# Seven quadrant products in fifteen column pairs of the up projection instead of eight

## The chip, the cores and the metric

The kernel runs on one core of one Trainium2 chip. The metric is the device time of one execution in microseconds, the median over several executions. The engines are TensorE (PE; its weight loads are PEld), VectorE (DVE), ScalarE (ACT), GpSimd (POOL) and SyncE (SP), which issues the transfers.

## The reference, cut to what matters

One layer of a decoder trunk for 512 tokens of width 1024 in float32. The change touches one product of it, the up projection of the channel-mixing part, whose output has 2 x 2816 columns:

```python
u = jnp.einsum('bsd,df->bsf', x, w_up[l])          # (512 x 1024) @ (1024 x 5632)
u_gate, u_val = jnp.split(u, 2, axis=-1)
a = jax.nn.gelu(causal_depthwise_conv(u_gate, w_conv[l], b_conv[l]), approximate=False) * u_val
ffn = jnp.einsum('bsf,fd->bsd', a, w_down[l])
```

## The kernel before

**Split products.** Every float32 operand of TensorE is held as a high part (rounded by ScalarE to fp32r) and a low part (the rest, a subtraction). `split_product` (line 1279 issues its matmuls) makes three matmuls for each product: high by high, high by low, low by high. For the streamed weights ScalarE writes the high part, `w_hi`, and GpSimd the low part, `w_lo`, in two subtractions of 128x512 (line 465).

**The stream.** Weights come as blocks of 128x1024, 512 KB each, through four slots. SP issues the load of a block when `block_done` says that TensorE is through with the block four places ahead of it.

**Column pairs.** The up projection is cut into `FB` = 22 pairs, numbered f = 0 to 21. A pair is a gate block and an up block, each 1024 keys by 128 columns, for the same 128 columns. A plain pair (`plain_up` on TensorE) is 2 blocks x 8 key tiles x 3 matmuls = 48 matmuls with 512 tokens each. ScalarE then reads the gate bank with scale and bias (`gate_conv`, line 761), VectorE adds the other two taps (`taps`, line 1145, two instructions), ScalarE takes the gelu (line 768), and VectorE multiplies by the up bank into `aT` (line 1153 or 1162). `act_ready` counts these products and frees the banks.

**Seven products.** In eight pairs (f = 5, 7, ..., 19) the pair's product is cut into quadrants (gate or up columns, lower or upper half of the keys, left or right half of the tokens) and made from seven products with sums of quadrants, by the Strassen-Winograd scheme, in place of eight. Each of the seven is 4 key tiles x 3 matmuls = 12 matmuls with 256 tokens, so 84 for the pair. The token sums `s_*` are made once. For every such pair the other engines make:
- VectorE: four weight sums `t_raw` of 128x512 (`w_sum`, line 1210; both inputs lie in SBUF, the on-chip memory), in the order 1, 2, 4, 3, and four additions of partial results of 128x256, `ps` and `p_copy` (lines 1221 to 1227);
- ScalarE: the high parts `t_hi` of the four sums (line 781), four copies of partial results out of PSUM, the matmul's output memory (`copy`, line 801), and the high parts of the gate block (line 786) and of half the up block (line 791);
- GpSimd: the low parts `t_lo` of the four sums (line 511), and the low parts of three quadrants of the weights: `b11_lo` (line 517), a quarter of the up block into `w_hi` (line 520) and the second gate quarter (line 526).

TensorE takes the products in the order P1 (sum 1), P2 (`b11`), P3 (the second gate quarter), P4 (sum 2), P5 (up block), P6 (sum 3), P7 (sum 4).

A plain pair runs ahead of each of the eight in one loop body, in which the seven-product pair has its fixed slots (`GATE_SLOT`, `UP_SLOT`) and fixed banks. Sums 2, 4 and 3 of a seven-product pair are made while TensorE works on the plain pair ahead of it. `t_raw` and `t_lo` of a sum share their memory. Each engine takes its instructions strictly in the written order.

Of the kernel before, what the change touches and what calls it, by code (L numbers as in the profile page):

```python
# [21 lines left out]
P = 128  # L22
# [98 lines left out]
def layer(nc, xT, x_tok, w_stream, w_out, cols, rows, square, out):  # L121
# [90 lines left out]
    t_raw = {m: at(f"t_raw{m}", [P, 512], f32, area_a + (50 + 2 * m) * K) for m in range(1, 5)}  # L212
# [28 lines left out]
    def plain(ap):  # L241

        return ap.bitcast(f32)

    with ExitStack() as ctx:
# [60 lines left out]
        p_done, p_copied, b21_lo = sem("p_done"), sem("p_copied"), sem("b21_lo")  # L306
# [35 lines left out]
        GATE_SLOT, UP_SLOT = (N_UP + 2) % 4, (N_UP + 3) % 4  # L342
        C11, C21, C12, C22 = (ps[:, c:c + HALF] for c in (1024, 1024 + HALF, 3 * 512, 5 * 512))
# [11 lines left out]
        def _(sp):  # L355
# [73 lines left out]
            assert n_loop == S_END  # L429
            for n in range(N_UP + 4, N_UP + 4 + 4 * S_FROM):  # L430
                load_when_free(n)
            with sp.Fori(S_FROM, S_END) as i:
# [27 lines left out]
        def _(pool):  # L460
# [43 lines left out]
            for n in range(N_UP + 2, N_UP + 4 * S_FROM + 2):  # L504
                low(n, n % 4)
            def sum_low(i, m):

                pool.wait_ge(t_hi_done, 4 * i + (SUMS.index(m) + 1 - 4 * S_FROM))
                if m in (1, 2):
                    pool.wait_ge(t_summed, 4 * i + (m + 1))  # L510
# [12 lines left out]
            def up_low(i, more):
                sum_low(i, 1)
                pool.wait_ge(t_summed, 4 * i + 3)
                nc.gpsimd.tensor_tensor(w_lo[:, GATE_SLOT, 512:1024], w_raw[:, GATE_SLOT, 512:1024],
                                        plain(w_hi[:, GATE_SLOT, 512:1024]), ALU.subtract).then_inc(b21_lo, 1)
                for m in (2, 3, 4):
                    sum_low(i, m)
                for j in range(4, 6):  # L530
                    low(4 * i + (N_UP + j), (N_UP + j) % 4)
                if more:
                    quarters_low(i + 1)

            quarters_low(S_FROM)
            with pool.Fori(S_FROM, S_END - 1) as i:
                up_low(i, True)
            up_low(S_END - 1, False)
            first = N_UP + 4 * S_END + 2
# [12 lines left out]
        def _(act):  # L552
# [226 lines left out]
            def w_sum_high(i, m):  # L779
                act.wait_ge(t_summed, 4 * i + (SUMS.index(m) + 1))  # L780
                nc.scalar.activation(t_hi[m][:], t_raw[m][:], ACT.Copy).then_inc(t_hi_done, 1)  # L781

            def gate_high(i):
                arrived(None, GATE_SLOT, i + (N_UP + 2) // 4)
                act.wait_ge(block_done, 4 * i + (N_UP - 1))
                nc.scalar.activation(w_hi[:, GATE_SLOT, :], w_raw[:, GATE_SLOT, :], ACT.Copy).then_inc(hi_ready, 1)

            def up_quarter_high(i):
                arrived(None, UP_SLOT, i + (N_UP + 3) // 4)
                act.wait_ge(block_done, 4 * i + N_UP)  # L790
# [12 lines left out]
            def up_high(i, more):

                for m in SUMS[1:]:
                    w_sum_high(i, m)
                act.wait_ge(block_done, 4 * i + (N_UP + 1))
                gate_conv(2 * i, 0)
                copy(i, 0, C12)
                next_high(i, 4)  # L810
                copy(i, 1, C22)
                gate_gelu(2 * i, 0)
                next_high(i, 5)
                copy(i, 2, C22)
                copy(i, 3, C22)
                if more:
                    gate_high(i + 1)
                act.wait_ge(gate_done, i + (1 - S_FROM))
                gate_conv(2 * i + 1, 1)
                if more:  # L820
                    up_quarter_high(i + 1)
                    w_sum_high(i + 1, 1)
                gate_gelu(2 * i + 1, 1)
# [15 lines left out]
            plain_up(3)  # L839
            gate_high(S_FROM)  # L840
            up_quarter_high(S_FROM)
            w_sum_high(S_FROM, 1)
            with act.Fori(S_FROM, S_END - 1) as i:
                up_high(i, True)
            up_high(S_END - 1, False)
            high_in_order(N_DOWN - 2)
            high_in_order(N_DOWN - 1)
            act.wait_ge(p_done, 5 * N_S)
# [30 lines left out]
        def _(dve):  # L879
# [320 lines left out]
            def w_sum(i, m):  # L1200

                b11, b21 = (w_raw[:, GATE_SLOT, 512 * k:512 * (k + 1)] for k in range(2))
                b12, b22 = (w_raw[:, UP_SLOT, 512 * k:512 * (k + 1)] for k in range(2))
                a, b = {1: (b12, b11), 2: (b22, t_raw[1][:]), 4: (b21, t_raw[2][:]), 3: (b22, b12)}[m]
                if m == 1:
                    for slot in (GATE_SLOT, UP_SLOT):
                        dve.wait_ge(raw_in[slot], 16 * i + (16 * ((N_UP + 2 + (slot == UP_SLOT)) // 4) + 16))
                else:
                    dve.wait_ge(t_summed, 4 * i + SUMS.index(m))
                nc.vector.tensor_tensor(t_raw[m][:], a, b, ALU.subtract).then_inc(t_summed, 1)  # L1210

            def up_products(i, more):

                count = i + (1 - S_FROM)
                for m in SUMS[1:]:
                    w_sum(i, m)
                taps(2 * i, 0)
                times_up(2 * i, 0, block_done, 4 * i + (N_UP + 2))
                dve.wait_ge(p_copied, 4 * i + (3 - 4 * S_FROM))
                dve.wait_ge(block_done, 4 * i + (N_UP + 4))  # L1220
                nc.vector.tensor_tensor(C12, C12, p_copy[:, 2, :], ALU.add).then_inc(up_left, 1)
                dve.wait_ge(p_copied, 4 * i + (4 - 4 * S_FROM))
                nc.vector.tensor_tensor(C22, C22, p_copy[:, 0, :], ALU.add).then_inc(up_right, 1)
                dve.wait_ge(p_done, 5 * i + (5 - 5 * S_FROM))
                nc.vector.tensor_tensor(C11, C11, p_copy[:, 1, :], ALU.add).then_inc(gate_left, 1)
                dve.wait_ge(gate_left, count)
                nc.vector.tensor_tensor(C21, C21, p_copy[:, 3, :], ALU.add).then_inc(gate_done, 1)
                if more:
                    w_sum(i + 1, 1)
                taps(2 * i + 1, 1)  # L1230
                times_halves(2 * i + 1, count)
# [444 lines left out]
```

## Time and profile before

| | us |
|---|---|
| median of 3 executions (lowest, highest) | 740.76 (740.60, 740.86) |
| the profiled execution, its own time | 741.66 |
| its span from the first to the last instruction | 739.9 |
| TensorE busy | 729.7 (99%) |
| VectorE, ScalarE, GpSimd busy | 427.9, 366.6, 383.1 |

The seven-product stretch runs from 433.81 us (the first matmul of pair 5) to 590.75 us (the first of pair 20). Busy times of matmuls overlap, so their spacing is read from the starts in the timeline and not from the mean duration. GB/s and clocks are for the whole stretch that a row names.

### The profile page before, as it was taken

The numbers are of one execution on the slowest core, as the hardware profiler recorded it, in microseconds if no ns is written. First come the engines' busy times: TensorE is split into PE (matmuls) and PEld (weight loads), VectorE is DVE, ScalarE is ACT, GpSimd is POOL, SyncE is SP. The second block draws the span as 40 slices with busy tenths as digits, with TensorE's granted clock in tenths as the row PEclk, the third lists the DMA queues.
The fourth block names the chain that finished last, engine by engine and source line by source line (L and its number), as shares of the span: only waits on it lengthen the run. The fifth ranks groups of instructions, "written<-read, shape, count | busy, mean of one in ns | idle before, by whom it ended". The sixth has DMA issues, their size and how long they took to land.

```text
span 739.9 us, 10440 instructions
## 1 busy us (share of the span) xinstructions
PE 729.7 (99%) x3763; PEld 623.9 (84%) x3763; DVE 427.9 (58%) x609; ACT 366.6 (50%) x525; POOL 383.1 (52%) x268
## 2 busy tenths in 40 slices
PE   8999999999999999999999999999999999999995
PEld 6888888888888888888898898888999988888884
DVE  3329579879889674446568545555444442322567
ACT  4325786876787775661125344544445343323410
POOL 6645245525525434981007577666667652845800
PEclk9999999999999999999999999999999999999998
DMA  8323414214124213661003332232323327222002
GB/s 304 112 100 117 126 55 112 90 58 143 58 80 119 86 58 140 258 231 54 0 1 114 106 123 85 85 108 90 113 85 113 113 86 284 99 100 85 28 29 85
DMA packets 24480, 78.36 MB, mean 106 GB/s; under 512 B 2944, under 2 KB 3328, under 8 KB 24448
## 3 DMA queue, kind: packets, MB, share of 16 engines
q1 hardware_dynamic: 24448, 77.94, 31.2%
q8 instruction: 20, 0.33, 0.2%
q14 instruction: 12, 0.10, 0.0%
HBM read 71.63 MB, written 2.10 MB: 100 GB/s over the span
## 4 chain that ended last, share of the span: by engine, by line
PE 94%; ACT 2%; DVE 2%; issue 1%; DMA 0%; POOL 0%; DVEq 0%; SPq 0%; POOLq 0%
PE ps L1279 92%; PE ps L1381 2%; PE ps L1462 0%; DMA w_raw<-w_stream_in 0%; POOL w_lo L465 0%; ACT fx_p L664 0%; DVE fx_p L988 0%; DVE sb_t L997 0%; DVE sb_lo L881 0%; DVE sb_t L1028 0%; ACT k_bias_rows L614 0%; ACT sb_t L658 0%; DVE fx_p L1025 0%; ACT sb_hi L688 0%; ACT sb_t L653 0%
## 5 line engine op out<-in xcount | busy, mean ns | idle before, releaser
L465 POOL TENSOR_TENSOR w_lo<-w_raw,w_hi 128x512 fp32r<-128x512 f32 x186 | 260.1, 1425 | 267.8 <-ACT w_hi L568 261.6
L568 ACT ACTIVATE w_hi<-w_raw 128x1024 fp32r<-128x1024 f32 x92 | 97.0, 1056 | 106.9 <-DMA w_raw<-w_stream_in 106.5
L1279 PE MATMUL ps<-x1T_hi,w_hi 128*128 128x512 f32 (+1 forms) x312 | 109.7, 352 | 0.0
L1279 PE MATMUL ps<-x1T_lo,w_hi 128*128 128x512 f32 (+1 forms) x312 | 109.6, 351 | 0.0
L1279 PE MATMUL ps<-xT_hi,w_hi 128*128 128x512 f32 x264 | 105.2, 399 | 0.0
L1279 PE MATMUL ps<-xT_lo,w_hi 128*128 128x512 f32 x264 | 102.9, 390 | 0.0
L1279 PE MATMUL ps<-x1T_hi,w_lo 128*128 128x512 f32 (+1 forms) x280 | 100.4, 359 | 0.0
L1279 PE MATMUL ps<-xT_hi,w_lo 128*128 128x512 f32 x256 | 100.0, 391 | 0.0
L881 DVE TENSOR_TENSOR a_lo<-aT,a_hi 128x512 fp32r<-128x512 f32 x22 | 32.9, 1511 | 64.2 <-ACT a_hi L756 64.2
L1279 PEld LDWEIGHTS ps<-x1T_hi,w_hi 128*128 128x128 f32 x312 | 59.1, 189 | 7.7
L1279 PEld LDWEIGHTS ps<-x1T_lo,w_hi 128*128 128x128 f32 x312 | 59.1, 189 | 7.4
L1279 PEld LDWEIGHTS ps<-x1T_hi,w_lo 128*128 128x128 f32 x280 | 52.9, 189 | 7.9
L1279 PEld LDWEIGHTS ps<-xT_lo,w_hi 128*128 128x128 f32 x264 | 49.7, 188 | 9.4
L1279 PEld LDWEIGHTS ps<-xT_hi,w_hi 128*128 128x128 f32 x264 | 49.6, 188 | 9.3
L1279 PEld LDWEIGHTS ps<-xT_hi,w_lo 128*128 128x128 f32 x256 | 48.0, 188 | 10.2
L1279 PE MATMUL ps<-w_hi,a_hi 128*128 128x512 f32 x136 | 52.9, 389 | 0.0
L1279 PE MATMUL ps<-w_lo,a_hi 128*128 128x512 f32 x136 | 52.9, 389 | 0.0
L1279 PE MATMUL ps<-w_hi,a_lo 128*128 128x512 f32 x136 | 52.9, 389 | 0.0
L511 POOL TENSOR_TENSOR t_lo<-t_raw,t_hi 128x512 fp32r<-128x512 f32 x32 | 44.8, 1420 | 15.3 <-DVE t_raw L1210 15.3
L1145 DVE SCALAR_TENSOR_TENSOR conv<-ps,col,conv 128x511 f32<-128x511 f32 (+1 forms) x44 | 32.9, 748 | 31.7 <-ACT conv L761 29.4
L801 ACT ACTIVATE p_copy<-ps 128x256 f32<-128x256 f32 x32 | 12.3, 385 | 50.5 <-PE ps L1279 49.6
L781 ACT ACTIVATE t_hi<-t_raw 128x512 fp32r<-128x512 f32 x32 | 20.2, 630 | 20.9 <-DVE t_raw L1210 20.1
(193 smaller groups left out, 1563.6 us busy)
## 6 DMA issues: line engine op xcount, KB each, us to landing
w_raw<-w_stream_in SPq DMA_DIRECT2D x109, 512.0 KB, 3.2
wout_raw<-w_out_in SPq DMA_DIRECT2D x8, 512.0 KB, 4.7
r_raw<-w_stream_in SPq DMA_DIRECT2D x5, 512.0 KB, 9.2
xT_raw<-xT_in SPq DMA_DIRECT2D x8, 256.0 KB, 7.0
x<-x_tok_in SPq DMA_DIRECT2D x4, 512.0 KB, 4.1
ln_rows<-rows_in SPq DMA_DIRECT2D x4, 512.0 KB, 5.7
out_dram<-x SPq DMA_DIRECT2D x8, 256.0 KB, 2.0
sb_q<-sb_q SPq DMA_DIRECT2D x8, 128.0 KB, 2.4
```

The source lines that it names most:

```text
L465: lo = nc.gpsimd.tensor_tensor(w_lo[:, slot, cs], w_raw[:, slot, cs], plain(w_hi[:, slot, cs]), ALU.subtract)
L511: nc.gpsimd.tensor_tensor(t_lo[m][:], t_raw[m][:], plain(t_hi[m][:]), ALU.subtract).then_inc(t_split, 1)
L568: nc.scalar.activation(w_hi[:, slot, :], w_raw[:, slot, :], ACT.Copy).then_inc(hi_ready, 1)
L781: nc.scalar.activation(t_hi[m][:], t_raw[m][:], ACT.Copy).then_inc(t_hi_done, 1)
L801: nc.scalar.activation(p_copy[:, k, :], place, ACT.Copy).then_inc(p_copied, 1)
L881: return nc.vector.tensor_tensor(out_lo, whole, plain(part_hi), ALU.subtract)
L1145: nc.vector.scalar_tensor_tensor(conv[:, j, t:SEQ], ps[:, 512 * 2 * j:512 * (2 * j + 1) - t], col[:, ds(f * CONV_WIDTH + (COL_CW + CONV_WI ...
L1279: return nc.tensor.matmul(out_, lhs, rhs, start=start, stop=stop, skip_group_check=True)
L1381: last = nc.tensor.transpose(ps[:, o:o + P], weights[:, QUERY_OFF[r] + P * c:QUERY_OFF[r] + P * (c + 1)], ident[:])
```

## The change

All fifteen pairs f = 5 to 19 are made with seven products. Banks and slots follow from f (`quarters_of`, `slot_of`): even and odd pairs have bank sets of their own. `t_raw` has memory of its own, and so has the low part of the second gate quarter (`b21_lo`). The loops now cover four pairs a round, three rounds (f = 6 to 17), with the rest written out. In the new bodies ScalarE (`up_high`), VectorE (`up_products`) and GpSimd (`up_low`, `seven_low`) work for three pairs in turn: the one before (f0 - 1), the present one (f0) and the next (f0 + 1). The final multiplication is two instructions of 256 tokens. GpSimd makes the low part of `b11` for pair f0 + 1 after P3 of pair f0 is done, since `b11_lo` is one buffer.

The core of the diff, mostly the added side; the replaced functions are those printed above:

```diff
+S_FIRST, S_LAST, ROUND = 5, 19, 4
+LOOP = S_FIRST + 1
+ROUNDS = (S_LAST + 1 - LOOP) // ROUND
...
+def by_seven(f):
+    return S_FIRST <= f <= S_LAST
+def sevens_ahead(f):
+    return sum(map(by_seven, range(f)))
+N_S = sevens_ahead(FB)
...
+    t_raw = {m: at(f"t_raw{m}", [P, 512], f32, area_g + (14 + 2 * m) * K) for m in range(1, 5)}
...
+    b21_lo = at("b21_lo", [P, 512], f32r, area_c)
...
+        def block_of(f0, i):
+            return 8 * i + (N_UP + 2 * f0)
+        def count_of(f0, i, each, k=0):
+            return ROUND * each * i + (each * sevens_ahead(f0) + k)
+        def slot_of(f0, g):
+            return (N_UP + 2 * f0 + g) % 4
+        def turn_of(f0, i, g):
+            return 2 * i + (N_UP + 2 * f0 + g) // 4
+        def quarters_of(f0):
+            j = f0 % 2
+            starts = 1024 * j, 1024 * j + HALF, 1024 * j + 512, (4 + j) * 512
+            return (ps[:, c:c + HALF] for c in starts)
...
+            def sum_low(f0, i, m):
+                pool.wait_ge(t_hi_done, count_of(f0, i, 4, m))
                 nc.gpsimd.tensor_tensor(t_lo[m][:], t_raw[m][:], plain(t_hi[m][:]),
                                         ALU.subtract).then_inc(t_split, 1)
...
+            def seven_low(g0, i):
+                gate, up = slot_of(g0, 0), slot_of(g0, 1)
+                pool.wait_ge(hi_ready, block_of(g0, i) + 1)
+                if by_seven(g0 - 1):
+                    pool.wait_ge(block_done, block_of(g0 - 1, i) + 1)
+                nc.gpsimd.tensor_tensor(b11_lo[:], w_raw[:, gate, 0:512], plain(w_hi[:, gate, 0:512]),
+                                        ALU.subtract).then_inc(lo_ready, 1)
+                pool.wait_ge(hi_ready, block_of(g0, i) + 2)
+                nc.gpsimd.tensor_tensor(w_hi[:, up, 0:512], w_raw[:, up, 512:1024], plain(w_hi[:, up, 512:1024]),
+                                        ALU.subtract).then_inc(lo_ready, 1)
+                sum_low(g0, i, 1)
+                nc.gpsimd.tensor_tensor(b21_lo[:], w_raw[:, gate, 512:1024], plain(w_hi[:, gate, 512:1024]),
+                                        ALU.subtract).then_inc(b21_split, 1)
+                sum_low(g0, i, 2)
+            def up_low(f0, i):
+                if by_seven(f0):
+                    sum_low(f0, i, 3)
+                    sum_low(f0, i, 4)
+                if by_seven(f0 + 1):
+                    seven_low(f0 + 1, i)
+                else:
+                    for g in range(2):
+                        low(block_of(f0 + 1, i) + g, slot_of(f0 + 1, g))
+            pool.sem_inc(t_split, 4)
+            for f in range(LOOP):
+                up_low(f, 0)
...
+            def w_sum_high(f0, i, m):
+                act.wait_ge(t_summed, count_of(f0, i, 4, SUMS.index(m) + 1))
+                act.wait_ge(p_done, count_of(f0, i, 5, (1, 3, 4, 5)[m - 1]))
                 nc.scalar.activation(t_hi[m][:], t_raw[m][:], ACT.Copy).then_inc(t_hi_done, 1)
...
+            def next_high(f0, i, g):
+                slot = slot_of(f0, g)
+                own = slice(512, 1024) if g == 1 and by_seven(f0) else slice(0, 1024)
+                arrived(None, slot, turn_of(f0, i, g))
+                act.wait_ge(block_done, block_of(f0, i) + (g - 3))
+                nc.scalar.activation(w_hi[:, slot, own], w_raw[:, slot, own], ACT.Copy).then_inc(hi_ready, 1)
+            def copy(f0, i, k, place):
+                act.wait_ge(p_done, count_of(f0, i, 5, 6 + k))
                 nc.scalar.activation(p_copy[:, k, :], place, ACT.Copy).then_inc(p_copied, 1)
...
+            def up_high(f0, i):
+                before, now, after = map(by_seven, (f0 - 1, f0, f0 + 1))
+                c11, c21, c12, c22 = quarters_of(f0)
+                last = 4 * i + (f0 - 1)
+                if now:
+                    w_sum_high(f0, i, 4)
+                if before:
+                    act.wait_ge(gate_done, count_of(f0 - 1, i, 1, 1))
+                else:
+                    act.wait_ge(block_done, block_of(f0 - 1, i) + 1)
+                gate_conv(last, (f0 - 1) % 2)
+                if now:
+                    copy(f0, i, 0, c12)
+                    copy(f0, i, 1, c22)
+                gate_gelu(last, (f0 - 1) % 2)
+                next_high(f0 + 1, i, 0)
+                if now:
+                    copy(f0, i, 2, c22)
+                next_high(f0 + 1, i, 1)
+                if after:
+                    w_sum_high(f0 + 1, i, 1)
+                    w_sum_high(f0 + 1, i, 2)
+                if now:
+                    copy(f0, i, 3, c22)
+                if after:
+                    w_sum_high(f0 + 1, i, 3)
...
+            def times_halves(f, j, count):
...
+                _, _, c12, c22 = quarters_of(j)
+                for t, ready, part in ((0, up_left, c12), (1, up_right, c22)):
+                    dve.wait_ge(ready, count)
+                    cs = slice(HALF * t, HALF * (t + 1))
+                    half_done = nc.vector.tensor_tensor(aT[:, ds(f, 1), cs].rearrange("p o c -> p (o c)"), part,
+                                                        gelu[:, j, cs], ALU.mult)
+                half_done.then_inc(act_ready, 1)
...
+            def w_sum(f0, i, m):
+                gate, up = slot_of(f0, 0), slot_of(f0, 1)
+                b11, b21 = (w_raw[:, gate, 512 * k:512 * (k + 1)] for k in range(2))
+                b12, b22 = (w_raw[:, up, 512 * k:512 * (k + 1)] for k in range(2))
...
+                    for g in range(2):
+                        dve.wait_ge(raw_in[slot_of(f0, g)], 16 * turn_of(f0, i, g) + 16)
...
+                    dve.wait_ge(t_summed, count_of(f0, i, 4, SUMS.index(m)))
+                dve.wait_ge(t_split, count_of(f0, i, 4, m))
                 nc.vector.tensor_tensor(t_raw[m][:], a, b, ALU.subtract).then_inc(t_summed, 1)
...
+            def up_products(f0, i):
+                before, now, after = map(by_seven, (f0 - 1, f0, f0 + 1))
+                last, j = 4 * i + (f0 - 1), (f0 - 1) % 2
+                if before:
+                    c11, c21, _, _ = quarters_of(f0 - 1)
+                    dve.wait_ge(p_done, count_of(f0 - 1, i, 5, 10))
+                    nc.vector.tensor_tensor(c11, c11, p_copy[:, 1, :], ALU.add).then_inc(gate_left, 1)
+                    dve.wait_ge(gate_left, count_of(f0 - 1, i, 1, 1))
+                    nc.vector.tensor_tensor(c21, c21, p_copy[:, 3, :], ALU.add).then_inc(gate_done, 1)
+                taps(last, j)
+                if after:
+                    w_sum(f0 + 1, i, 1)
+                if before:
+                    times_halves(last, j, count_of(f0 - 1, i, 1, 1))
+                else:
+                    times_up(last, j, block_done, block_of(f0 - 1, i) + 2)
+                if after:
+                    w_sum(f0 + 1, i, 2)
+                    w_sum(f0 + 1, i, 4)
+                _, _, c12, c22 = quarters_of(f0)
+                if now:
+                    dve.wait_ge(p_copied, count_of(f0, i, 4, 3))
+                    dve.wait_ge(block_done, block_of(f0, i) + 2)
+                    nc.vector.tensor_tensor(c12, c12, p_copy[:, 2, :], ALU.add).then_inc(up_left, 1)
+                if after:
+                    w_sum(f0 + 1, i, 3)
+                if now:
+                    dve.wait_ge(p_copied, count_of(f0, i, 4, 4))
+                    nc.vector.tensor_tensor(c22, c22, p_copy[:, 0, :], ALU.add).then_inc(up_right, 1)
...
+                pe.wait_ge(act_ready, 4 * i + (f0 + 1))
...
+                    up(block_of(f0, i) + g, slot_of(f0, g), 2 * (f0 % 2) + g, 0, SEQ)
+            def seven_products(f0, i):
...
+                def sum_ready(m):
+                    pe.wait_ge(t_split, count_of(f0, i, 4, m + 4))
...
+                    pe.wait_ge(p_copied, count_of(f0, i, 4, k))
+                c11, c21, c12, c22 = quarters_of(f0)
+                gate, up_ = slot_of(f0, 0), slot_of(f0, 1)
+                pe.wait_ge(act_ready, 4 * i + (f0 + 1))
...
+                times(c12, t_hi[1], t_lo[1], s_hi[1], s_lo[1], True).then_inc(p_done, 1)
+                weight_ready(block_of(f0, i))
+                times(c22, w_hi[:, gate, 0:512], b11_lo, *x_parts(0, 0), True).then_inc(p_done, 1)
+                pe.wait_ge(b21_split, count_of(f0, i, 1, 1))
+                pe.wait_ge(t_summed, count_of(f0, i, 4, 3))
+                times(c11, w_hi[:, gate, 512:1024], b21_lo, *x_parts(1, 0), True).then_inc(block_done, 1)
...
+                times(c22, t_hi[2], t_lo[2], s_hi[2], s_lo[2]).then_inc(p_done, 1)
+                weight_ready(block_of(f0, i) + 1)
+                pe.wait_ge(t_summed, count_of(f0, i, 4, 4))
+                times(c12, w_hi[:, up_, 512:1024], w_hi[:, up_, 0:512], s_hi[4], s_lo[4]).then_inc(block_done, 1)
...
+                times(c22, t_hi[3], t_lo[3], s_hi[3], s_lo[3]).then_inc(p_done, 1)
...
+                times(c21, t_hi[4], t_lo[4], *x_parts(1, 1)).then_inc(p_done, 1)
...
+            def next_up(f0, i=0):
+                if by_seven(f0):
+                    seven_products(f0, i)
+                else:
+                    plain_up(f0, i)
+            for f in range(2, S_FIRST):
+                plain_up(f)
+            pe.sem_inc(p_done, 5)
+            seven_products(S_FIRST, 0)
+            with pe.Fori(0, ROUNDS) as i:
+                for f in range(LOOP, LOOP + ROUND):
+                    next_up(f, i)
+            for f in range(LOOP + ROUND * ROUNDS, FB):
+                next_up(f)
...
```

## Rows read from the trace of the kernel before

**Rows 1.** The page: busy time by engine, and the chain that ended last.
```profile
PE 729.7 (99%) x3763; PEld 623.9 (84%) x3763; DVE 427.9 (58%) x609; ACT 366.6 (50%) x525; POOL 383.1 (52%) x268
...
PE 94%; ACT 2%; DVE 2%; issue 1%; DMA 0%; POOL 0%; DVEq 0%; SPq 0%; POOLq 0%
```

**Rows 2.** Windows: a seven-product pair, then a plain pair; columns in the first row.
```profile
core 0: us, PE busy (x) PEld busy (x) DVE busy (x) ACT busy (x) POOL busy (x), PEclk, DMA share, GB/s
475.77:485.85 10.08, 10.08 (x86) 10.07 (x84) 2.31 (x4) 4.81 (x8) 7.58 (x7) 1.00 0.45 154
485.85:496.75 10.90, 10.90 (x50) 9.01 (x49) 7.67 (x10) 5.11 (x9) 7.32 (x6) 1.00 0.16 50
```

**Rows 3.** Timeline, TensorE: start us, duration us, instruction; both kinds of spacing.
```profile
485.61 0.28 PE L1279 MATMUL ps<-x1T_lo,t_hi 128*128 128x256 f32 x1
485.73 0.28 PE L1279 MATMUL ps<-x1T_hi,t_lo 128*128 128x256 f32 x1
485.85 0.40 PE L1279 MATMUL ps<-x1T_hi,w_hi 128*128 128x512 f32 x1
```

**Rows 4.** Timeline, GpSimd, 484 to 500 us; idle before and its releaser in brackets.
```profile
486.02 1.30 POOL L517 TENSOR_TENSOR b_lo<-w_raw,w_hi 128x512 fp32r<-128x512 f32 x1 [2.15 <-ACT w_hi L786]
...
492.02 1.80 POOL L511 TENSOR_TENSOR t_lo<-t_raw,t_hi 128x512 fp32r<-128x512 f32 x1 [2.09 <-DVE t_raw L1210]
493.78 1.74 POOL L526 TENSOR_TENSOR w_lo<-w_raw,w_hi 128x512 fp32r<-128x512 f32 x1
495.48 3.81 POOL L511 TENSOR_TENSOR t_lo<-t_raw,t_hi 128x512 fp32r<-128x512 f32 x3
```

**Rows 5.** Timeline, VectorE, 426 to 428 us and 485 to 498 us.
```profile
426.53 0.69 DVE L1210 TENSOR_TENSOR t_raw<-w_raw 128x512 f32<-128x512 f32 x1 [2.63 <-DMA w_raw<-w_stream_in]
...
486.05 0.43 DVE L1225 TENSOR_TENSOR ps<-ps,p_copy 128x256 f32<-128x256 f32 x1 [0.59 <-PE ps L1279]
486.51 0.43 DVE L1227 TENSOR_TENSOR ps<-ps,p_copy 128x256 f32<-128x256 f32 x1
486.86 1.00 DVE L1210 TENSOR_TENSOR t_raw<-w_raw 128x512 f32<-128x512 f32 x1
488.20 1.64 DVE L1145 SCALAR_TENSOR_TENSOR conv<-ps,col,conv 128x511 f32<-128x511 f32 x2 [0.34 <-ACT conv L761]
490.65 0.69 DVE L1162 TENSOR_TENSOR aT<-ps,gelu 128x512 f32 x1 [0.81 <-ACT gelu L768]
491.26 1.41 DVE L1210 TENSOR_TENSOR t_raw<-w_raw,t_raw 128x512 f32<-128x512 f32 x2
492.70 1.67 DVE L1210 TENSOR_TENSOR t_raw<-w_raw 128x512 f32<-128x512 f32 x1
495.86 1.64 DVE L1145 SCALAR_TENSOR_TENSOR conv<-ps,col,conv 128x511 f32<-128x511 f32 x2 [1.49 <-ACT conv L761]
```

**Rows 6.** Timeline, ScalarE, 484 to 490 us.
```profile
484.61 0.39 ACT L801 ACTIVATE p_copy<-ps 128x256 f32<-128x256 f32 x1 [2.50 <-PE ps L1279]
484.89 1.05 ACT L786 ACTIVATE w_hi<-w_raw 128x1024 fp32r<-128x1024 f32 x1
487.26 0.78 ACT L761 ACTIVATE conv<-ps,col 128x512 f32<-128x512 f32 x1 [1.33 <-DVE ps L1227]
487.94 0.62 ACT L791 ACTIVATE w_hi<-w_raw 128x512 fp32r<-128x512 f32 x1
488.46 0.62 ACT L781 ACTIVATE t_hi<-t_raw 128x512 fp32r<-128x512 f32 x1
489.88 0.63 ACT L768 ACTIVATE gelu<-conv 128x512 f32<-128x512 f32 x1 [0.79 <-DVE conv L1145]
```

**Rows 7.** Timeline, GpSimd in the down projection: two halves without and with `a_lo`.
```profile
606.13 2.54 POOL L465 TENSOR_TENSOR w_lo<-w_raw,w_hi 128x512 fp32r<-128x512 f32 x2 [1.74 <-ACT w_hi L568]
...
639.05 2.99 POOL L465 TENSOR_TENSOR w_lo<-w_raw,w_hi 128x512 fp32r<-128x512 f32 x2 [0.99 <-ACT w_hi L568]
```

**Rows 8.** The page: weight loads, KB each, median us to landing.
```profile
w_raw<-w_stream_in SPq DMA_DIRECT2D x109, 512.0 KB, 3.2
```

More of the change, by code:

```diff
@@ L428, in _ @@
             n_loop = (N_DOWN + 3 - N_UP - 4) // 4
[L429 to L432, printed above, removed]
+            with sp.Fori(0, n_loop) as i:
                 for j in range(4):
@@ L523, in up_low @@
[L523 to L539, printed above, removed]
+            def seven_low(g0, i):
[12 more added lines that the diff above has]
+                sum_low(g0, i, 2)
@@ new lines, in up_low @@
+            def up_low(f0, i):
[10 more added lines that the diff above has]
+                up_low(f, 0)
+            with pool.Fori(0, ROUNDS) as i:
+                for f in range(LOOP, LOOP + ROUND):
+                    up_low(f, i)
@@ L540, in _ @@
+            for f in range(LOOP + ROUND * ROUNDS, S_LAST + 2):
+                up_low(f, 0)
+            first = N_UP + 2 * S_LAST + 6
             n_loop = (N_RESIDENT - first) // 4
@@ L838, in _ @@
             high_in_order(N_UP + 9)
[L839 to L848, printed above, removed]
+            for f in range(S_FIRST - 1, LOOP):
+                up_high(f, 0)
+            with act.Fori(0, ROUNDS) as i:
+                for f in range(LOOP, LOOP + ROUND):
+                    up_high(f, i)
+            for f in range(LOOP + ROUND * ROUNDS, S_LAST + 2):
+                up_high(f, 0)
+            act.wait_ge(p_done, 5 * N_S + 5)
             a_high(0, 0)
@@ L1210, in w_sum @@
+                dve.wait_ge(t_split, count_of(f0, i, 4, m))
                 nc.vector.tensor_tensor(t_raw[m][:], a, b, ALU.subtract).then_inc(t_summed, 1)
[L1212 to L1231, printed above, removed]
@@ L1251, in _ @@
             x_sum_low(4)
-            plain_up(3)
-            dve.sem_inc(t_summed, 4 * S_FROM)
-            w_sum(S_FROM, 1)
-            with dve.Fori(S_FROM, S_END - 1) as i:
-                up_products(i, True)
-            up_products(S_END - 1, False)
+            for f in range(S_FIRST - 1, LOOP):
+                up_products(f, 0)
+            with dve.Fori(0, ROUNDS) as i:
+                for f in range(LOOP, LOOP + ROUND):
+                    up_products(f, i)
+            for f in range(LOOP + ROUND * ROUNDS, S_LAST + 2):
+                up_products(f, 0)
             a_low(0, 0)
@@ L1536, in seven_products @@
+                c11, c21, c12, c22 = quarters_of(f0)
+                gate, up_ = slot_of(f0, 0), slot_of(f0, 1)
+                pe.wait_ge(act_ready, 4 * i + (f0 + 1))
                 pe.wait_ge(s_split, 4)
                 sum_ready(1)
-                times(C12, t_hi[1], t_lo[1], s_hi[1], s_lo[1], True).then_inc(p_done, 1)
-                weight_ready(4 * i + (N_UP + 2))
-                times(C22, w_hi[:, GATE_SLOT, 0:512], b11_lo, *x_parts(0, 0), True).then_inc(p_done, 1)
-                pe.wait_ge(b21_lo, i + (1 - S_FROM))
@@ L1557, in _ @@
-            for f in range(2, 2 * S_FROM):
-                plain_up(f, f % 2)
-            with pe.Fori(S_FROM, S_END) as i:
-                plain_up(2 * i, 0)
-                seven_products(i)
-            for f in range(FB - 2, FB):
-                plain_up(f, f % 2)
+                times(c21, t_hi[4], t_lo[4], *x_parts(1, 1)).then_inc(p_done, 1)
[4 more added lines that the diff above has]
+                    plain_up(f0, i)
@@ L1566, in down @@
+            for f in range(2, S_FIRST):
[3 more added lines that the diff above has]
+            with pe.Fori(0, ROUNDS) as i:
+                for f in range(LOOP, LOOP + ROUND):
+                    next_up(f, i)
+            for f in range(LOOP + ROUND * ROUNDS, FB):
+                next_up(f)
             def down(s, half_, f, slot_a, w_part_hi, w_part_lo, slot_w):
```

88 lines of the change are left out of this document (2 added, 86 removed).

## The prediction

> **What bounds the kernel now.** I read the page first. TensorE is busy 99% of the span and the chain that ended last is PE for 94% [rows 1], so only what TensorE does or waits for counts. Then windows on one loop body: seven products take 10.08 us, a plain pair 10.90 us, both without a gap and at a granted clock of 1.00 [rows 2]. The starts are 0.12 us apart with 256 tokens [rows 3] and 10.90 / 48 = 0.23 us with 512. Next, who works beside it: GpSimd is busy 7.58 + 7.32 = 14.9 of 20.98 us [rows 2]. Last, the timelines of the three helpers [rows 4 to 6]: they prepare a seven-product pair during the 10.90 us of the plain pair ahead, and the first sum's low part is ready at 493.82, 2.9 us before TensorE takes it at 496.75.
>
> **What the change removes on TensorE.** Seven of the fifteen pairs go from 48 matmuls to 84 short ones: 10.90 - 10.08 = 0.82 us each, 5.7 us in all, if TensorE never waits. The stretch is now 8 x 10.08 + 7 x 10.90 = 156.9 us (433.81 to 590.75) and would be 151.2. By the Trainium skill (TensorE: Matmul & The Clock Gate, Back-to-back issue gap: columns / 2.4 + 2.5 ns) the pair would win 48 x 215.8 - 84 x 109.2 ns = 1.19 us; the trace's 0.82 decides.
>
> **What it adds on GpSimd.** A seven-product pair needs seven subtractions of 128x512: three quadrants and four sums. Three in a row take 3.81, so one follows the other after (3.81 - 1.30) / 2 = 1.255 us; seven are 8.8 us in every 10.08, where two pairs had 11 in 20.98. That alone fits.
>
> **What stands beside it on VectorE.** Both engines stretch when a `w_sum` (two SBUF inputs) meets a GpSimd subtraction. A sum alone takes 0.69; the one at 486.86 takes 1.00 and ends 0.54 after GpSimd's instruction, the one at 492.70 takes 1.67 and ends at 494.37, 0.55 after GpSimd's at 493.82 [rows 4, 5]. GpSimd's instruction behind a sum takes 1.80 and 1.74 for 1.30, as if it began 0.15 before the sum's end [rows 4, 5]. They take turns, and a meeting costs GpSimd 0.44 to 0.50; `a_lo`, with the same kind of inputs, makes 2.99 of 2.54 [rows 7]. I take 0.45. Additions with a PSUM input, and the taps, do not meet anything: 0.43 and 1.64 beside GpSimd's 1.30 and 3.81 [rows 4, 5]. With all four sums meeting, GpSimd needs 8.8 + 1.8 = 10.6 us a pair: already over 10.08, though below 10.90. With the plain pairs gone, no stretch is left in which GpSimd catches up.
>
> The Trainium skill (SBUF — State Buffer, SBUF: two separate sides) says that the pair of ports shared by the two engines is an exclusive lock, held for the whole instruction, and (A bandwidth-pool intuition that's wrong) that the blocked one starts some 115 ns after the other's end. By that a meeting would cost 0.69 + 0.12 = 0.81 us and GpSimd 12.0 us a pair, worse than plain; the trace has 0.45.
>
> **The order of one new pair.** Each engine is strictly in order, so I lay one round out from row durations. Zero is the start of VectorE's addition into `c11` of the pair before. `c21` starts at 0.46 and ends at 0.89; ScalarE's conv begins 0.32 later (486.94 to 487.26), 1.21 to 1.99; the taps begin 0.16 later and take 1.64, to 3.79; gelu 3.83 to 4.46 [rows 5, 6]. Only then does `up_high` turn to the next gate block: its high part starts 0.52 after gelu's start (487.94 to 488.46 is that spacing for the same size) and takes 1.05, 4.35 to 5.40; GpSimd follows 0.08 later (485.94 to 486.02), so `b11` runs 5.48 to 6.78 [rows 4, 6]. This late start is what the new order brings: before, the gate block came ahead of conv.
> The next three GpSimd steps are `b11`, `b22`, sum 1's low part, and VectorE's sums 2, 4 and 3 fall between them. Sum 2 waits for `b11` and ends at 6.78 + 0.55 = 7.33. `b22` ends at 7.33 - 0.15 + 1.30 = 8.48, sum 4 at 9.03, sum 1's low part at 10.18, sum 3 at 10.73. VectorE's `c12` addition fits between sums 4 and 3. After sum 3 come `c22` (10.65, since an instruction follows 0.08 before the end of one that it needn't wait for) and, 0.35 later (486.51 to 486.86), `c11` again: **one round is 11.0 us**. TensorE takes sum 1 at about 10.18 + 0.08 = 10.26 and so starts every 11.0 us, waiting 0.9 us a pair. The rest is in time: from TensorE's start the low part of the second gate quarter is ready at 1.6 (wanted at 2.9), sum 2 at 2.9 (4.3), sum 3 at 4.1 (7.2), sum 4 at 5.4 (8.6). ScalarE's copies, about 0.28 each, wait for P1, P2, P4 and P6 and are not last. Loads land in 3.2 us [rows 8], after a slot is freed 4.3 or 7.2 us into a pair and a whole pair before use; SP is passed by nothing new. `b21_lo` and `t_raw` only move; the first takes one 1.30 as before.
>
> **Does sum 2 come before or after `b11`?** That decides. Sum 1 is issued at 3.71. In the round above sum 1's low part is followed by the second gate quarter (to 11.88), sum 2 (13.14), sum 3 (14.39) and sum 4 (15.65), that is 4.65 in the next round. So `w_sum` 1 meets sum 4's low part and ends at 5.20. The two half multiplications follow; the trace has no such row, so I bound them by 2 x 0.35 from the 256-token additions and 2 x 0.61 (490.65 to 491.26) from the whole one, and take the nearest, 0.70. Sum 2 is then issued at 5.8 or later, behind `b11` at 5.48. The order holds itself, with 0.3 us in hand.
>
> **The first rounds.** Pair 5 is prepared in plain pair 4 and starts on time. For pair 6 the up block lands at 3.4 us, w_sum 1 ends at 4.1, sum 2 comes ahead of `b11`, and sum 1's low part is done at 10.05: pair 6 starts after 10.13. In pair 6, `w_sum` 1 is issued at 3.86 and GpSimd began sum 4's low part at 3.65, so it is blocked, and pair 7 starts after 10.41. Pairs 7 to 18 take 11.0 each. Pair 19 prepares a plain pair, without sums: 10.08.
>
> **Sum.** 10.13 + 10.41 + 12 x 11.0 + 10.08 = 162.6 against 156.9: +5.7 us. The profiled execution took 741.66 (span 739.9 and 1.8 around it) and gives 747.3; it lies 0.9 above the median of the runs, so the forecast is 740.76 + 5.7 = **746.4 us**. Register instructions ahead of a wait are in the gaps 0.32 and 0.16; if a new one is added at each of the ring's handovers, the round is longer: bounded by 0 and 0.32, I take 0, and 11.3 as the far end (+3.6).
>
> **The rivals.**
> (a) The other turn: `w_sum` 1 meets sum 3's low part and not sum 4's, ends at 4.4, and sum 2 is issued at 5.3, before `b11`. Then sum 1's low part comes after two meetings and sum 3 leaves the ring; GpSimd's own 10.56 bounds. 10.13 + 12 x 10.56 + 10.41 + 10.08 = 157.3, +0.4: 741.2, no change. For it: pair 6 misses this by only 0.2 us. Against: once late, the round keeps itself late. 0.20.
> (b) The other side: the sums mostly find GpSimd idle, or less meets than I count, and the helpers keep up: 151.2 to 154, 735 to 738 us. It decides if a round falls under 10.4. GpSimd with only three meetings has 10.15, and would need to be idle never; the late gate block speaks against it. 0.20.
> (c) The two engines exclude each other for whole instructions: GpSimd begins only at a sum's end and a sum only at GpSimd's. The two full turns and the last half turn of the ring would grow by about 0.4, 0.4 and 0.14, a round of 11.95, +17 us: 757.8. The 1.74 and 1.80 for a blocked GpSimd instruction [rows 4] speak against. 0.03. This is the lock as the Trainium skill's page SBUF — State Buffer states it, above.
> (d) Handovers cost more (register work in larger loop bodies): 750 to 753. 0.07.
> The forecast has 0.50, with a range of its own from 743 to 750.
>
> **How the numbers follow.** Below the range of 736.5 to 750.5 lies half of (b), above it (c) and most of (d): under 0.2. A measurement of this kernel tells 0.2% (1.5 us) from no change. Faster is (b), 0.2, with a little of (a); of (a) most is no change, 0.17; slower is the forecast, (c), (d) and the upper edge of (a): 0.62.
>
> **What would show it.** TensorE without work ahead of the first matmul with sum 1 in pairs 7 to 18, for 0.9 us, released by GpSimd's `t_lo`; pairs 11.0 us apart; the P1 to P7 of a pair still 10.08. `w_sum` 2 released after `b11` and lasting over 1 us; sums of 1.2 to 1.7 us and `t_lo` or `b22` of 1.74 in every pair. GpSimd busy about 10.1 of 11.0. Pairs 10.08 apart would refute the ring, pairs 10.5 would show (a), a meeting above 0.7 us (c). The weakest steps are the issue of sum 2 against `b11`, and the 0.32 ahead of conv.

## The result and the profile after

The changed kernel takes 747.5 us (median of six executions, 747.25 to 749.34) against 740.87 of the kernel before (six, 740.60 to 741.94). The ratio is 1.0086, 95% interval 1.0076 to 1.0096: 6.4 us slower by the ratio (the medians lie 6.6 apart), where 5.7 had been forecast.

The page of the changed kernel, for comparison with [rows 1]: TensorE's busy time falls by a single microsecond and its share by two points, and the chain that ended last now runs through other engines too.

```profile
PE 728.7 (97%) x4015; PEld 633.6 (85%) x4015; DVE 483.1 (65%) x680; ACT 389.0 (52%) x581; POOL 420.4 (56%) x289
...
PE 76%; DVE 8%; issue 7%; POOL 4%; ACT 3%; DMA 1%; DVEq 1%; ACTq 0%; SPq 0%; POOLq 0%
```

The waits between 433 and 600 us, engine line waited for: us in total, times, longest. TensorE waits for one thing only.

```profile
PE ps L1327 <- POOL t_lo L536: 8.2, 13, 0.7
```

TensorE's timeline around the start of two neighbouring pairs. The last matmul of a pair starts at 499.25 or 510.33, the first of the next at 500.27 or 511.24. The pair between takes 10.97 us, and at its two ends 1.02 and 0.91 us lie between neighbouring starts, where 0.12 would follow without a wait.

```profile
499.25 0.28 PE L1327 MATMUL ps<-x1T_hi,t_lo 128*128 128x256 f32 x1
500.27 0.39 PE L1327 MATMUL ps<-s_hi,t_hi 128*128 128x256 f32 x1 [0.75 <-POOL t_lo L536]
...
510.33 0.28 PE L1327 MATMUL ps<-x1T_hi,t_lo 128*128 128x256 f32 x1
511.24 0.39 PE L1327 MATMUL ps<-s_hi,t_hi 128*128 128x256 f32 x1 [0.63 <-POOL t_lo L536]
```

The same pair in the windows view, the columns of [rows 2]: GpSimd is busy 10.16 of 10.97 us and VectorE 9.28, TensorE 10.34. The clock is still 1.00.

```profile
500.27:511.24 10.97, 10.34 (x84) 10.14 (x84) 9.28 (x13) 6.53 (x12) 10.16 (x8) 1.00 0.30 96
```

Now one round on the three helpers, that is one turn of the work that repeats with each pair, VectorE first. It answers to [rows 5]; the round starts with the addition into `c11` at 501.03 and ends with the next one at 512.00.

```profile
501.03 0.42 DVE L1256 TENSOR_TENSOR ps<-ps,p_copy 128x256 f32<-128x256 f32 x1
501.48 0.43 DVE L1258 TENSOR_TENSOR ps<-ps,p_copy 128x256 f32<-128x256 f32 x1
503.17 1.64 DVE L1179 SCALAR_TENSOR_TENSOR conv<-ps,col,conv 128x511 f32<-128x511 f32 x2 [1.26 <-ACT conv L796]
504.73 1.52 DVE L1247 TENSOR_TENSOR t_raw<-w_raw 128x512 f32<-128x512 f32 x1
506.17 0.74 DVE L1197 TENSOR_TENSOR aT<-ps,gelu 128x256 f32 x2
506.84 1.52 DVE L1247 TENSOR_TENSOR t_raw<-w_raw,t_raw 128x512 f32<-128x512 f32 x1
508.61 1.45 DVE L1247 TENSOR_TENSOR t_raw<-w_raw,t_raw 128x512 f32<-128x512 f32 x1 [0.25 <-DVE t_raw L1247]
509.98 0.42 DVE L1273 TENSOR_TENSOR ps<-ps,p_copy 128x256 f32<-128x256 f32 x1
510.32 1.42 DVE L1247 TENSOR_TENSOR t_raw<-w_raw 128x512 f32<-128x512 f32 x1
511.66 0.42 DVE L1278 TENSOR_TENSOR ps<-ps,p_copy 128x256 f32<-128x256 f32 x1
512.00 0.42 DVE L1256 TENSOR_TENSOR ps<-ps,p_copy 128x256 f32<-128x256 f32 x1
```

GpSimd in the same round, for [rows 4]: `b11`, the up quarter, sum 1's low part, the second gate quarter.

```profile
506.51 1.30 POOL L545 TENSOR_TENSOR b_lo<-w_raw,w_hi 128x512 fp32r<-128x512 f32 x1 [0.81 <-ACT w_hi L826]
507.77 1.74 POOL L548 TENSOR_TENSOR w_hi<-w_raw,w_hi 128x512 fp32r<-128x512 f32 x1
509.48 1.71 POOL L536 TENSOR_TENSOR t_lo<-t_raw,t_hi 128x512 fp32r<-128x512 f32 x1
511.15 1.75 POOL L551 TENSOR_TENSOR b_lo<-w_raw,w_hi 128x512 fp32r<-128x512 f32 x1
```

And ScalarE, for [rows 6]: conv behind `c21`, gelu behind the taps, and only then the gate block's high part, for which GpSimd has waited 0.81 us.

```profile
502.23 0.78 ACT L796 ACTIVATE conv<-ps,col 128x512 f32<-128x512 f32 x1 [0.27 <-DVE ps L1258]
...
504.85 0.63 ACT L803 ACTIVATE gelu<-conv 128x512 f32<-128x512 f32 x1 [1.01 <-DVE conv L1179]
505.39 1.04 ACT L826 ACTIVATE w_hi<-w_raw 128x1024 fp32r<-128x1024 f32 x1
```

In this round all four weight sums last 1.42 to 1.52 us in place of 0.69, and the three GpSimd instructions that begin behind one last 1.71 to 1.75 in place of 1.30; the remaining sum (504.73) waits for a subtraction, behind which GpSimd has nothing ready. Counted from 501.03, the round laid out beforehand and the measured one are:

| step | forecast | measured |
|---|---|---|
| conv starts | 1.21 | 1.20 |
| gelu starts | 3.83 | 3.82 |
| `b11` starts | 5.48 | 5.48 |
| sum 2 issued, done | 5.8, 7.33 | 5.81, 7.33 |
| sum 4 done | 9.03 | 9.03 |
| sum 1's low part done | 10.18 | 10.16 |
| TensorE starts the next pair | 10.26 | 10.21 |
| sum 3 done | 10.73 | 10.71 |
| next `c11` | 11.0 | 10.97 |

The starts of all pairs, read from TensorE's timeline, give these distances (the stretch from pair 5 to pair 20):

| kernel | pair 5 to 6, 6 to 7 | the rest | stretch |
|---|---|---|---|
| before | 10.08, 10.91 | in turn | 156.9 |
| forecast | 10.13, 10.41 | 12 x 11.0, 10.08 | 162.6 |
| after | 10.15, 10.50 | 12 between 10.96 and 11.08, 10.15 | 162.8 |

The stretch explains 5.9 of the 6.4 us; the other 0.5 lies outside the stretch and is within the interval of the ratio (0.7 us either way), so it is not explained. The profiled execution of the changed kernel took 749.34 us, the longest of the six: it reached pair 5, the last one ahead of the change, at 435.61, where the kernel before reached it at 433.81.

From pair 10 to 11 and from pair 14 to 15 the distance is 11.08, 0.1 us more than between their neighbours. In both rounds `b11` starts 0.16 us behind the end of its high part and not 0.08 (at 495.53 and 539.51). They lie four pairs apart, as the turns of the loop do; that the turn of the loop is the cause was not tried.

### The profile page after: what moved, and what is told of

It is laid out like the page before. It is cut to its first block, busy times and chain, and to the rows that moved or that the text cites. A ratio compares the mean times of both kernels' runs of the same rounds, so it can differ in the third digit from the quotient of the medians.

```text
span 747.5 us, 11297 instructions
## 1 busy us (share of the span) xinstructions
PE 728.7 (97%) x4015; PEld 633.6 (85%) x4015; DVE 483.1 (65%) x680; ACT 389.0 (52%) x581; POOL 420.4 (56%) x289
## 4 chain that ended last, share of the span: by engine, by line
PE 76%; DVE 8%; issue 7%; POOL 4%; ACT 3%; DMA 1%; DVEq 1%; ACTq 0%; SPq 0%; POOLq 0%
PE ps L1327 73%; DVE t_raw L1247 4%; POOL t_lo L536 2%; PE ps L1429 2%; DVE conv L1179 1%; ACT conv L796 1%; POOL b_lo L551 1%; ACT t_hi L818 1%; POOL b_lo L545 1%; DVE aT L1197 1%; DMA w_raw<-w_stream_in 1%; PE ps L1510 0%; POOL w_hi L548 0%; ACT fx_p L699 0%; DVE fx_p L1022 0%
## 5 line engine op out<-in xcount | busy, mean ns | idle before, releaser
L495 POOL TENSOR_TENSOR w_lo<-w_raw,w_hi 128x512 fp32r<-128x512 f32 x158 | 225.0, 1448 | 263.9 <-ACT w_hi L603 251.5
L603 ACT ACTIVATE w_hi<-w_raw 128x1024 fp32r<-128x1024 f32 x74 | 78.3, 1059 | 107.4 <-DMA w_raw<-w_stream_in 107.0
L536 POOL TENSOR_TENSOR t_lo<-t_raw,t_hi 128x512 fp32r<-128x512 f32 x60 | 82.9, 1403 | 2.2 <-ACT t_hi L818 2.2
L1327 PE MATMUL ps<-x1T_hi,w_hi 128*128 128x256 f32 (+1 forms) x256 | 81.9, 320 | 0.0
L1327 PE MATMUL ps<-x1T_lo,w_hi 128*128 128x256 f32 (+1 forms) x256 | 81.8, 320 | 0.0
L1327 PE MATMUL ps<-s_hi,t_hi 128*128 128x256 f32 x180 | 52.3, 291 | 8.2 <-POOL t_lo L536 8.2
L818 ACT ACTIVATE t_hi<-t_raw 128x512 fp32r<-128x512 f32 x60 | 35.9, 626 | 37.1 <-DVE t_raw L1247 33.5
L1327 PEld LDWEIGHTS ps<-x1T_hi,w_hi 128*128 128x128 f32 x256 | 48.8, 191 | 3.5
L1327 PE MATMUL ps<-s_hi,t_lo 128*128 128x256 f32 x180 | 50.9, 283 | 0.0
L1327 PE MATMUL ps<-s_lo,t_hi 128*128 128x256 f32 x180 | 50.9, 283 | 0.0
```

Source lines behind the costliest of these rows:

```text
L495: lo = nc.gpsimd.tensor_tensor(w_lo[:, slot, cs], w_raw[:, slot, cs], plain(w_hi[:, slot, cs]), ALU.subtract)
L603: nc.scalar.activation(w_hi[:, slot, :], w_raw[:, slot, :], ACT.Copy).then_inc(hi_ready, 1)
L1327: return nc.tensor.matmul(out_, lhs, rhs, start=start, stop=stop, skip_group_check=True)
```

## Experiments

All change the changed kernel. "Before" was timed beside them on the same chips, at medians of 741.37 to 741.78 us.

**Without meetings.** The second operand of every weight sum comes from an idle bank of PSUM, so the sums hold other values than they should.

```diff
-                nc.vector.tensor_tensor(t_raw[m][:], a, b, ALU.subtract).then_inc(t_summed, 1)
+                nc.vector.tensor_tensor(t_raw[m][:], a, bank(7), ALU.subtract).then_inc(t_summed, 1)
```

> The second operand of all four weight sums is read from a bank of PSUM that nothing else uses at that time, so the sums hold other values than they should; number, size and order of all instructions stay. My theory (a weight sum with two inputs in SBUF and a GpSimd subtraction take turns, and this stretches the round of c11, c21, conv, taps, gelu, gate block, b11, b22, sum 1, sum 3, c22 to 11.0 us): every weight sum takes about 0.7 us, GpSimd's subtractions 1.30, seven of them 8.8 us a pair, TensorE takes a pair every 10.08 us, and the time is about 735.5 us (ratio to before 0.993). Rival (GpSimd's seven subtractions, or register work in the longer loop bodies, are the limit by themselves): pairs stay near 11.0 us and the time near 747.

735.84 us, ratio 0.9923 (0.9906 to 0.9939). Fifteen pairs, each after 10.07 or 10.08 us; the stretch is 151.2 us. The groups between 433.86 and 585.05 us, first GpSimd, then VectorE (line, names, shapes, count; busy us, mean ns): every subtraction is back at 1300 ns and every weight sum at 680.

```profile
L548 POOL TENSOR_TENSOR w_hi<-w_raw,w_hi 128x512 fp32r<-128x512 f32 x14 | 18.2, 1300 | 1.1 <-ACT w_hi L826 1.1
```

```profile
L1247 DVE TENSOR_TENSOR t_raw<-w_raw,ps 128x512 f32<-128x512 f32 x56 | 38.1, 680 | 5.2 <-DMA w_raw<-w_stream_in 3.1 <-DVE t_raw L1247 1.0
```

Not one instruction fewer, the same loops, the same late gate block: the rival, load or register work by themselves, is out. Without the meetings nothing of the loss is left.

**The gate block first.**

```diff
                 if now:
                     w_sum_high(f0, i, 4)
+                next_high(f0 + 1, i, 0)
                 if before:
                     act.wait_ge(gate_done, count_of(f0 - 1, i, 1, 1))
...
                 gate_gelu(last, (f0 - 1) % 2)
-                next_high(f0 + 1, i, 0)
```

> ScalarE makes the high part of the next gate block ahead of conv and gelu, as the kernel before did. My theory: b11 starts as soon as GpSimd is through with sum 4's low part, about 0.8 us earlier in the round; then GpSimd's own work with four meetings, 7 x 1.255 + 4 x 0.45 = 10.6 us, is the limit, pairs come every 10.5 to 10.6 us and the time is about 741.5 us (ratio 1.001). Rival A (the late gate block is the whole loss): pairs of 10.1 us, 735 to 736. Rival B (the place of the gate block does not matter, since the meetings alone make 11.0): unchanged, 747.

742.17 us, ratio 1.0006 (0.9996 to 1.0015): level with the kernel before. From the third distance to the fourteenth they are 10.52 to 10.69 us, most of them 10.58. The windows view over two pairs shows what limits them: GpSimd is busy 21.17 of 21.17 us.

```profile
496.39:517.56 21.17, 20.68 (x168) 20.27 (x168) 16.80 (x25) 12.77 (x24) 21.17 (x15) 1.00 0.28 99
```

Both rivals are out; the late gate block is a link of the round, and behind the round stands GpSimd's own pace.

**Sum 3 a round later.**

```diff
+                if now:
+                    w_sum(f0, i, 3)
                 taps(last, j)
...
-                if after:
-                    w_sum(f0 + 1, i, 3)
```

(ScalarE's high parts of sums 3 and 4 go behind conv.)

> VectorE makes sum 3 of a pair in the next round, behind the additions into c11 and c21, and ScalarE the high parts of sums 3 and 4 behind conv, so that sum 3 no longer stands between sum 1's low part and c22. The gate block stays late. My theory: the round loses this step (10.73 - 9.03 = 1.7 us), TensorE's next pair hangs on b11, b22 and sum 1 alone, and GpSimd's 10.6 us becomes the limit: 10.5 to 10.7 us a pair, 741 to 743 us. Rival (sum 3 is not in the round that sets the pace; the late gate block and GpSimd are): 11.0 us, 747.

743.1 us, ratio 1.0022 (1.0011 to 1.0032). Pairs of mostly 10.58 us, GpSimd without a pause, after one of 11.19 (pair 6 to 7), which I had not forecast: GpSimd stood idle 1.38 us there, waiting for the later high part of a sum. Sum 3 is a link of the round too.

**Both cuts.** The moves of the last two experiments together; ScalarE's part is

```diff
-                if now:
-                    w_sum_high(f0, i, 4)
+                next_high(f0 + 1, i, 0)
...
                 gate_conv(last, (f0 - 1) % 2)
                 if now:
+                    w_sum_high(f0, i, 3)
+                    w_sum_high(f0, i, 4)
                     copy(f0, i, 0, c12)
```

> The gate block ahead of conv and sum 3 in the next round, both at once. My theory: either cut alone already brought the pair to GpSimd's own pace, 7 x 1.255 + 4 x 0.45 = 10.58 us, so the two together give nothing more: 10.58 us a pair, 742 us (ratio 1.001). Rival (the 10.58 us of the two single cuts were each a shorter chain through VectorE and ScalarE that happened to be as long): 10.1 to 10.3 us a pair, 735 to 738 us.

743.08 us, ratio 1.0021 (1.0011 to 1.003), pairs of mostly 10.58, again after one of 11.14 (pair 6 to 7). Two cuts give no more than one; over 478 to 499 us GpSimd has no idle time.

```profile
478.00:499.00 21.00, 20.52 (x169) 20.11 (x169) 17.02 (x25) 12.79 (x25) 21.00 (x15) 1.00 0.30 101
```

**Sum 2 ahead of the half multiplications.** The prediction named this order as the point that decides.

```diff
                 if after:
                     w_sum(f0 + 1, i, 1)
+                    w_sum(f0 + 1, i, 2)
...
                 if after:
-                    w_sum(f0 + 1, i, 2)
                     w_sum(f0 + 1, i, 4)
```

> VectorE makes sum 2 directly behind sum 1, ahead of the two half multiplications; all else stays, the late gate block too. All is computed. My theory (it decides whether sum 2 meets GpSimd ahead of b11 or behind it): sum 2 is issued at about 5.2 us of the round, ahead of b11 at 5.5; sum 4 then meets b11, sum 3 meets b22, and VectorE is back at c11 before P7 is done. GpSimd's own pace is left, 7 x 1.255 + 4 x 0.45 = 10.6 us a pair, 742 to 743 us (rival (a) of the prediction, made on purpose). Rival (the four meetings cost the same wherever they fall, the order does not matter): pairs of 11.0 us, 747.

742.79 us, ratio 1.0019 (1.0009 to 1.0029). Pairs of 10.56 to 10.66 us from the third distance to the fourteenth. Sum 2 is issued at 512.31, and GpSimd's `b11` starts at 513.29 behind it and lasts 1.77; VectorE's two halves follow at 513.82.

```profile
511.43 0.76 DVE L1247 TENSOR_TENSOR t_raw<-w_raw 128x512 f32<-128x512 f32 x1
512.31 1.59 DVE L1247 TENSOR_TENSOR t_raw<-w_raw,t_raw 128x512 f32<-128x512 f32 x1
513.82 0.74 DVE L1197 TENSOR_TENSOR aT<-ps,gelu 128x256 f32 x2
...
513.29 1.77 POOL L545 TENSOR_TENSOR b_lo<-w_raw,w_hi 128x512 fp32r<-128x512 f32 x1
```

The same instructions and the same late gate block, one of them moved past two of 0.4 us, bring the ratio from 1.0086 down to 1.0019, though GpSimd now loses time in four meetings a pair and not in three. The number of meetings is not enough to tell the time; which of them lie on the round is.

**Three meetings.** The gate block first, and sum 3 alone with its second operand from PSUM (it holds other values than it should).

```diff
+                nc.vector.tensor_tensor(t_raw[m][:], a, bank(7) if m == 3 else b, ALU.subtract).then_inc(t_summed, 1)
```

> The gate block ahead of conv, and the second operand of sum 3 alone read from an unused bank of PSUM (sum 3 holds other values). Three meetings a pair are left. My theory: GpSimd's pace is 7 x 1.255 + 3 x 0.45 = 10.13 us; pairs of 10.1 to 10.2 us, 735.5 to 737 us. If a meeting cost GpSimd nothing it would be 10.58 as before, if the whole sum of 0.69 and more, below 10.08 and hidden behind TensorE, which the timeline of GpSimd tells apart (idle time ahead of b11).

736.82 us, ratio 0.9941 (0.9926 to 0.9956), pairs of 10.12 to 10.21 us from the fourth distance on. The number is as forecast, its reason is not. GpSimd:

```profile
509.45 1.75 POOL L545 TENSOR_TENSOR b_lo<-w_raw,w_hi 128x512 fp32r<-128x512 f32 x1
511.55 1.35 POOL L548 TENSOR_TENSOR w_hi<-w_raw,w_hi 128x512 fp32r<-128x512 f32 x1 [0.36 <-ACT w_hi L826]
512.86 1.75 POOL L536 TENSOR_TENSOR t_lo<-t_raw,t_hi 128x512 fp32r<-128x512 f32 x1
```

Only two meetings are full ones, and GpSimd idles 0.36 us a pair for the up quarter's high part. ScalarE makes that behind the copy after P4:

```profile
510.57 0.39 ACT L831 ACTIVATE p_copy<-ps 128x256 f32<-128x256 f32 x1 [1.05 <-PE ps L1327]
510.85 0.62 ACT L826 ACTIVATE w_hi<-w_raw 128x512 fp32r<-128x512 f32 x1
```

From TensorE's pair start at 504.54 over P4 (510.57), this high part, the up quarter and sum 1's low part (514.61) to the next start at 514.69 is 10.15 us: a second, shorter round, which the prediction had not laid out, with one meeting in it. So this run does not price a meeting; the 10.58 us of the four runs above, 7 x 1.255 + 4 x 0.45, does.

**The up block in PSUM.** ScalarE copies the raw up block into banks 6 and 7; sums 1, 2 and 3 read it there. All is computed.

```diff
+                b12, b22 = bank(6), bank(7)
+                if m == 3:
+                    b12 = w_raw[:, up, 0:512]
...
                 gate_conv(last, (f0 - 1) % 2)
+                if after:
+                    arrived(None, slot_of(f0 + 1, 1), turn_of(f0 + 1, i, 1))
+                    act.wait_ge(t_summed, count_of(f0 + 1, i, 4, 0))
+                    nc.scalar.activation(ps[:, 6 * 512:8 * 512], w_raw[:, slot_of(f0 + 1, 1), :],
+                                         ACT.Copy).then_inc(up_copied, 1)
```

> ScalarE copies the raw up block (128x1024) into two free banks of PSUM, behind conv, and VectorE's sums 1, 2 and 3 take it from there, so that only sum 4 has two inputs in SBUF. All is computed. My theory: one meeting a pair is left, GpSimd needs 8.8 + 0.45 = 9.2 us, sum 1's low part is done 9.8 us after c11, TensorE does not wait: pairs of 10.08 us and about 735.5 us (ratio 0.993). Rival 1 (ScalarE's extra copy of about 1.05 us lengthens the round through gelu and the gate block): 10.3 to 10.6 us a pair, 739 to 742. Rival 2 (meetings are not the cause): 747 or more.

737.44 us, ratio 0.9944 (0.9928 to 0.9961): pairs of 10.08 to 10.18 us, but 11.13 from pair 5 to 6. There ScalarE waits 3.65 us for the up block's load, and the copies of partial results, for which P4 waits, stand behind it:

```profile
437.33 1.03 ACT L849 ACTIVATE ps<-w_raw 128x1024 f32<-128x1024 f32 x1 [3.65 <-DMA w_raw<-w_stream_in]
438.29 0.64 ACT L832 ACTIVATE p_copy<-ps 128x256 f32<-128x256 f32 x2
```

I had costed the copy's 1.05 us and forgotten what is queued behind its wait in the one round in which the load is fresh.

**The same with that mended, and the gate block first.** In pair 5 the copy goes behind the two copies of partial results (`if f0 == S_FIRST`).

> The up block copied into PSUM for sums 1, 2 and 3, with the gate block ahead of conv, and in pair 5 alone the copy behind the two copies of partial results (it lost 1.05 us there by waiting for the up block's load). All is computed. My theory: one meeting, GpSimd 9.2 us a pair, no wait on TensorE in any of the fifteen pairs: 151.2 to 151.6 us for the stretch, 735.3 us, ratio 0.9925. Rival (the copy of 1.05 us ahead of the copies of partial results still delays P4 or P6 by a few hundredths a pair): 10.11 a pair, 735.8.

735.44 us, ratio 0.9923 (0.9909 to 0.9936), about 5.7 us less than the kernel before and 12 less than the changed one. All fifteen pairs come after 10.07 or 10.08 us. Over two pairs TensorE has no gap, GpSimd is busy 18.24 of 20.16 us and VectorE 12.90:

```profile
492.86:513.02 20.16, 20.16 (x170) 20.16 (x169) 12.90 (x24) 14.43 (x26) 18.24 (x15) 1.00 0.31 103
```

Of the versions that compute everything it is the fastest, ahead of both kernels.

**Twelve pairs.** Pairs 8, 12 and 16 plain, the gate block first, everything else as in the changed kernel (`count_of` counts three such pairs a round).

```diff
-    return S_FIRST <= f <= S_LAST
+    return S_FIRST <= f <= S_LAST and f % 4 != 0
```

> Twelve pairs by seven products, with plain pairs 8, 12 and 16 between them, and the gate block ahead of conv. All is computed. My theory: GpSimd has 31.4 us of subtractions and 5.4 us of meetings in four pairs, against 41.1 us of TensorE, and catches up in each plain pair; a group of three starts its pairs after 10.11, 10.16 and 10.14 us as the first ones of the last gate-first run did. 12 x 10.14 + 3 x 10.90 = 154.4 us against 156.9: 738.3 us, ratio 0.9966. Rival (the backlog does not clear within one plain pair, since each low part has one buffer): the second and later groups lose about 0.5 us a pair, 741 us or more.

739.52 us, ratio 0.9974 (0.9964 to 0.9984). The first group's pairs come after 10.11, 10.17 and 10.16 us, the later ones after 10.23 to 10.32, 10.17 to 10.26 and 10.13 or 10.14: one plain pair clears nearly all of the backlog. The stretch is 154.9 us, 0.5 more than forecast.

## Why the prediction was right

**TensorE's gain.** 0.82 us a pair and 5.7 in all, if it never waits: [rows 2] gave it, and the run without meetings and the one with the up block in PSUM and the gate block first measure it, 151.2 us for the stretch in each.

**GpSimd's load and the meeting.** 1.255 us a subtraction and 0.45 a meeting add up to 10.58 a pair; four runs that break the round in different places all settle at 10.58 with GpSimd busy throughout. The exclusive lock that the Trainium skill describes (SBUF — State Buffer, SBUF: two separate sides) is borne out as to who meets whom: reading one operand from PSUM ends it. Its price of a whole instruction is not: GpSimd's instruction is 0.45 us longer behind a sum of 0.69, and rival (c) with 11.95 us a round did not come. The price given to that rival was too high by its own rows: a full turn would grow by 0.15 for GpSimd's later start and 0.14 for the sum's, 0.29 and not 0.4, which makes a round of 11.7. That did not come either.

**The round.** 11.0 us forecast, 10.96 to 11.08 measured, step by step as in the table. Three links were cut one at a time (the gate block, sum 3, the order of sum 2), and each time the round gave way to GpSimd's 10.58.

**Sum 2 behind `b11`.** Issued at 5.81 against 5.48, as laid out. Putting it first made rival (a), 1.4 us above the kernel before where the prediction had 0.4; the stretch was 158.1 us where 157.3 was forecast, of which 0.45 is one early pair (10.86 for 10.41) and most of the rest 10.58 for 10.56.

**The first rounds.** 10.13 and 10.41 against 10.15 and 10.50. **The handovers** inside a round took what the rows gave; only 0.1 us in two rounds four pairs apart came on top, so (d) did not come. **Rival (b)** failed on its condition: with all four sums meeting and no plain pair between, no round settles under 10.4; without meetings it is the result.

## What to carry to other kernels

When plain work between heavy pieces is taken out, add up each helper's work for one piece against the piece's new length, and then lay out one round in each engine's strict order: the busy shares here (56% for GpSimd, 65% for VectorE over the whole span) show neither limit. Where VectorE and GpSimd meet, what counts is which meetings lie on the round back to the first instruction; here one reordered instruction bought 5 us, and the up block moved to PSUM together with a reorder 12 us. Whoever moves a wait ahead in a strict queue should check the first round by itself, where the load is still on its way.

## What the runs showed of the hardware

A VectorE instruction of 128x512 with one operand in PSUM and one in SBUF takes 0.68 us and neither delays nor is delayed by GpSimd, whose subtraction stays at 1.30 beside it (the run without meetings); with both in SBUF it takes 1.42 to 1.52 in the round shown, where it waits for a subtraction. ScalarE's copy of 128x1024 from SBUF into PSUM takes 1.03 us, as long as its high part into SBUF (1.04). On GpSimd's side 0.41 to 0.47 us is added in the rounds shown, less than the sum's 0.69. GpSimd's instruction ends 1.13 to 1.16 us after the sum that it waited for, though alone it takes 1.30, as if the two overlapped by some 0.15 us; why was not tried.
